# Start of a two-layer hybrid encoder: later release of the input loads, and six projections taken group by group

## What is computed

```
cond = silu(c)
mod  = cond @ w_ada[l] + b_ada[l]                    # 6 vectors of 1024 a layer: shift, scale, gate, twice
h = rms_norm(x, g_mix) * (1 + scale) + shift         # x: 2048 x 1024 a core, float32
q_a, k_a, v_a, q_b, k_b, v_b, f, q_c, k_c, v_c, gates = split(h @ w_in)
o_a = sliding-window attention with sinks and ALiBi (8 query heads, 2 key/value heads)
o_b = forgetting attention;  o_c = chunked attention with relative bias
x += gate * ((sigmoid(gates) * branch projections).sum() @ w_out)
h = rms_norm(x, g_ffn) * (1 + scale) + shift
x += gate * (silu(h @ w1) * (h @ w2)) @ w_ffn_out
```

## Time and profile before

| | |
|---|---|
| median of 3 runs (lowest to highest) | 2981.44 us (2753.49 to 3167.28) |
| the profiled execution, its own time | 2753.0 us |
| its span, slowest core (7) | 2751.4 us |
| spans of the eight cores | 2743.5 to 2751.4 us |
| TensorE, matmul busy | 2623.9 us (95%) |
| VectorE, ScalarE, POOL busy | 958.1, 984.3, 276.2 us |
| mean granted TensorE clock, core 7 | 0.982 |

### The profile page before, as it was taken

The page is one execution under the profiler, slowest core; times in us unless marked ns, Lnnn a source line. Parts: engine busy times, 40 slices in busy tenths (PEclk is TensorE's granted clock), DMA queues, the critical chain, the costliest instruction groups (busy, mean ns, idle before and its releaser), DMA issues.

```text
span 2751.4 us, 43022 instructions; the slowest of 8 cores (2743.5 to 2751.4 us)
## 1 busy us (share of the span) xinstructions
PE 2623.9 (95%) x16192; PEld 1197.6 (44%) x16192; DVE 958.1 (35%) x1423; ACT 984.3 (36%) x1326; POOL 276.2 (10%) x338
## 2 busy tenths in 40 slices
PE   1799999999999999999989999999999999999998
PEld 0234444454444444444434344454544444444443
DVE  1453221223444623223254422222244453232326
ACT  1356666554222520110143665654522243101012
POOL 1401000000000210000030100000000021000002
PEclk7799999999999999999999999999999999999999
DMA  9022222221233453343441100112032243222213
GB/s 214 16 35 48 44 48 38 54 30 18 35 45 65 111 88 64 51 76 59 70 140 25 20 13 17 18 41 41 15 50 35 41 115 62 39 39 39 39 31 123
DMA packets 66520, 148.11 MB, mean 54 GB/s; under 512 B 6592, under 2 KB 19456, under 8 KB 64272
## 3 DMA queue, kind: packets, MB, share of 16 engines
q0 software_dynamic: 55712, 99.76, 23.1%
q1 hardware_dynamic: 10608, 45.61, 4.7%
HBM read 228.12 MB, written 16.97 MB: 89 GB/s over the span
## 4 chain that ended last, share of the span: by engine, by line
PE 91%; DMA 3%; ACT 2%; DVE 2%; issue 2%; DVEq 0%; POOL 0%; POOLq 0%; ACTq 0%
PE ps L378 71%; PE ps L376 20%; DMA sb_WS<-wada 2%; ACT sb_PT L388 1%; DVE sb_TMPF L397 1%; ACT sb_HT L388 1%; DVE sb_XT L397 0%; DMA sb_WS<-win 0%; DMA sb_WS<-wfi 0%; DVE sb_RD L392 0%; ACT sb_TMPF L388 0%; ACT sb_RS L388 0%; DVE sb_W L401 0%; DVE sb_W L407 0%; ACT L388 0%
## 5 line engine op out<-in xcount | busy, mean ns | idle before, releaser
L378 PE MATMUL ps<-sb_HT,sb_WS 128*128 128x512 bf16 (+1 forms) x5760 | 1318.5, 383 | 43.0 <-ACT sb_HT L388 24.8
L378 PEld LDWEIGHTS ps<-sb_HT,sb_WS 128*128 128x128 bf16 (+1 forms) x5760 | 551.0, 98 | 725.0 <-issue 94.0
L388 ACT ACTIVATE sb_TMPF<-ps 128x512 f32<-128x512 f32 x388 | 231.6, 598 | 1140.8 <-PE ps L378 1137.4
L388 ACT ACTIVATE sb_PT<-ps 128x1024 bf16<-128x1024 f32 (+1 forms) x494 | 489.0, 990 | 404.3 <-PE ps L376 400.7
L378 PE MATMUL ps<-sb_W,sb_WS 128*128 128x512 bf16 x1920 | 418.0, 379 | 0.8 <-DVE sb_W L392 0.7
L392 DVE TENSOR_TENSOR sb_W<-ps,sb_TMPF 128x512 bf16<-128x512 f32 x176 | 121.4, 691 | 484.7 <-PE ps L378 472.7
L378 PEld LDWEIGHTS ps<-sb_W,sb_WS 128*128 128x128 bf16 x1920 | 187.5, 98 | 226.8 <-issue 1.8
L376 PE MATMUL ps<-sb_W 128*128 128x512 bf16 (+7 forms) x1212 | 256.1, 337 | 0.0
L407 DVE CAST sb_W<-ps 128x512 bf16<-128x512 f32 (+1 forms) x176 | 121.5, 690 | 386.0 <-PE ps L378 385.5
L397 DVE SCALAR_TENSOR_TENSOR sb_XT<-ps,sb_modT,sb_XT 128x512 f32<-128x512 f32 x256 | 186.5, 749 | 153.9 <-PE ps L378 153.7
L376 PE MATMUL ps<-sb_PT,sb_W 128*64 128x512 bf16 (+3 forms) x1212 | 197.0, 351 | 8.9 <-ACT sb_PT L388 7.6
(11 more groups left out here) (55 smaller groups left out, 1176.8 us busy)
## 6 DMA issues: line engine op xcount, KB each, us to landing
sb_WS<-wada POOLq DMA_DIRECT2D x48, 512.0 KB, 7.9
sb_WS<-wfi POOLq DMA_DIRECT2D x44, 512.0 KB, 5.3
sb_WS<-wmg POOLq DMA_DIRECT2D x48, 384.0 KB, 4.9
sb_XT<-x SPq DMA_DIRECT2D x8, 2048.0 KB, 18.2
sb_WS<-win POOLq DMA_DIRECT2D x60, 256.0 KB, 4.3
sb_WS<-wfo POOLq DMA_DIRECT2D x24, 512.0 KB, 5.3
xs<-sb_XT SPq DMA_DIRECT2D x4, 2048.0 KB, 6.6
sb_XT<-xs SPq DMA_DIRECT2D x4, 2048.0 KB, 17.1
```

Of the source, the lines that this page charges most:

```text
L378: r = e.matmul(o, lhsT=l, rhs=rr, start=st, stop=sp)
L388: return P.op("act", lambda e, o=out, i=in_, f=func, kw=kw: e.activation(out=o, in_=i, func=f, **kw), reads=reads, writes=writes)
```

## The change

Two things in one. First, the loads of x1, x2 and x3 no longer wait for the weights of blocks 4, 5 and 6 but all three for those of block 7, the eighth; SP issues them one behind the other. Second, `a_begin` takes all six units and `a_group` runs all six on a group, so K and V of a group come right after its Q and `a_rest` is gone. In layer 0 the norm of the next group is emitted inside the group: after the fourth projection in group 0, after the second in groups 1 and 2. In layer 1 no norm is emitted inside; group 3's norm still follows the first `a_group`, which is now six projections long. The six weights keep their order in the ring.

```diff
     def a_begin(l):
...
-        pro = [(c,) + w3(l * 30 + c, c > 0) for c in range(4)]
+        pro = [(c,) + w3(l * 30 + c, c > 0) for c in range(6)]
         return pro
...
-    def a_group(pro, g):
+    def a_group(pro, g, at=None, then=None):
         for (c, wv3, wb) in pro:
             bi = dbank()
-            drain(proj_fm(wv3, wb, g, bi))
-            ts(QA[:, c, sl(g)], PS[bi][:, :], 0.125, ALU.mult, [psb[bi]], [qab[c][g]])
-
-    def a_rest(l):
-        wv3, wb = w3(l * 30 + 4)
-        for g in range(NG):
-            bi = dbank()
-            drain(proj_fm(wv3, wb, g, bi))
-            copy("dve", KA[:, sl(g)], PS[bi][:, :], [psb[bi]], [kab[g]])
-        wv3, wb = w3(l * 30 + 5)
-        for t4 in range(4):
-            drain(proj_v(wv3, wb, t4, VA, vab, dbank()))
+            if c < 5:
+                drain(proj_fm(wv3, wb, g, bi))
+                if c < 4:
+                    ts(QA[:, c, sl(g)], PS[bi][:, :], 0.125, ALU.mult, [psb[bi]], [qab[c][g]])
+                else:
+                    copy("dve", KA[:, sl(g)], PS[bi][:, :], [psb[bi]], [kab[g]])
+            else:
+                drain(proj_v(wv3, wb, g, VA, vab, bi))
+            if c == at:
+                then()
...
     for jb in range(8):
         ada_block(0, jb)
-        if jb in (4, 5, 6):
+        if jb == 2:
+            norm_rs(0, sq)
+        if jb == 7:
             after = Buf()
             after.last_write = wsb[jb % NS].last_write
-            xload(jb - 3, x_d, [after])
-        if jb == 2:
-            norm_rs(0, sq)
+            for g in range(1, NG):
+                xload(g, x_d, [after])
...
-        a_group(pro, g)
-        if g + 1 < NG:
-            norm_fin(g + 1, sq, *mixv(0), pool=True)
+        a_group(pro, g, 3 if g == 0 else 1 if g + 1 < NG else None,
+                lambda g=g, sq=sq: norm_fin(g + 1, sq, *mixv(0), pool=True))
...
     for l in range(nl):
-        a_rest(l)
         run_steps(a_steps(l), a_filler(l), 104)
```

## The result

The changed kernel took 2721.22 us (median of 4 runs, 2720.34 to 2721.65). Of the runs of the kernel before, some were slowed by a lower clock on one die and are left out of every comparison; the undisturbed ones lie at 2751 to 2755. The ratio of after to before is 0.988, 95% interval 0.9856 to 0.9904: about 32 us faster, inside 2% and clear of no change. The profiled execution took 2720.9 us, its slowest core (2) 2719.3.

A forecast was written before the change was run, and what follows sets the result against it. Waits for conditioning weights, then idle or half-clock gaps at A's norms, were taken to bound the start. Block 7's 17.7 us and 14.8 from projections in the gaps gave -32.5: 2753.0 to 2720.5, say 2721 us, range 2709 to 2743.

The forecast's parts named there:

- Step 1, block 7: Before A: without x beside the conditioning weights, block 7 moves from 60.74 to 43 us, -17.7 (bounds -14.7 and -18.9).
- Step 1, x1's flight: Load of x1, issued at block 7's start: lands 16.5 us later, with 12 us as the other bound.
- Step 2, group 0: A's first group, us after block 7: first sum as if at +20.0, K and V hidden, second sum at +34.6.
- (b): A's own weights starve while x flows: fourth weight at +30, first sum 11.7 us later, time 2733 us; chance 0.09.
- the best case of 109: Whole phase: block 7 at 41.8, x1 after 12 us, no clock loss; phase ends at 109, time 2715 us.
- Step 2, the period: Groups 1 and 2: sums of squares 14.8 us apart instead of 19.7, TensorE idling 2.5 behind VectorE's scalings.
- The clock's term: Groups 1 and 2: 0.8 us of clock loss for two gaps of 2.5 us, bounds 0 and 5.2.
- Step 3: End of the A phase, a_rest gone: lost cover for memsets and loads costs nothing, 2 us if it fails.
- Step 4: Layer 1, six projections per group: the 8.22 us wait for a weight stays; effect 0, bounds -1 and +3 us.
- (a): x1 lands with x2 and x3, at +28 instead of +16.5; first sum onward 11.7 us later, 2733 us; chance 0.16.
- (c): Gain given back: x and weights still end at about 71, new gaps at half clock; 2744 to about 2753; chance 0.09.
- (d): Slower: x1 lands later as eight cores ask for 6 MB each at once; 2764 us if it takes 60; chance 0.04.

The follow-up runs named there:

- e3_stagger: The kernel after, but only x1 released by block 7; x2 held until K's weights have landed, x3 until V's; 2717.4 us (ratio 0.9874).
- e1_release_only: The kernel before with x1 to x3 all released by block 7, A's projections in the old order; 2735.8 us (ratio 0.9941).

## Why the prediction held, and where it did not

The forecast was 2721 us from the profiled execution's 2753.0; measured were 2721.2, and -32.5 us for the phase stands against -31.6 in the mean of the cores. Sign and place were right, and the period of groups 1 and 2 was right in its mechanism. The close size is in part luck: two terms were off and did not show.

The step that failed is the last of the sum: "A measurement of this kernel can tell about 2% (55 us) from no change, so the whole gain lies inside it." It took the 32 us that the steps before it had added up for no measurable change, and no row was given for the 2%. The runs showed that those of one kernel agree to 0.15% (2750.8 to 2754.7 for the kernel before, 2720.3 to 2721.7 for the kernel after), that the interval of the ratio is 0.5% wide (0.9856 to 0.9904), and that 1.2% is far outside it. The chance for "within 2%" held only because the gain is under that bound. Step by step:

- **Step 1, block 7.** Forecast at 43 from bounds of 41.8 to 46; measured 42.5 in the mean. The step was -17.7 on paper and is -16.1, since the core that was read had block 7 2.2 us later than the mean of the eight in the kernel before. That 43 was met is partly luck. The forecast gave three blocks 9 us from block 4's run at 33.94. They took 11.7 in the mean, 3.9 a block, which is the upper bound's 4.0 a landing and not the rate of q0 alone (7.9 for the three); but block 4 ran at 30.8 in the mean instead of 33.94. Block 5 came 5.4 us behind block 4, blocks 6 and 7 each 3.2 behind the one before.
- **Step 1, x1's flight.** I took the measured 16.5 us; it was 12.8 (12.6 to 13.2 over the cores), near the other bound. Term mis-sized by 3.7 us. Before, the shortest x load took 15.5 to 16.5 on every core, so it was not the core. A full weight queue and another x load close behind were there in both kernels and do not explain it. What differs is what the x queue had moved when x1 landed: 3.15 MB from 38 on before, 2.38 from 46 on after. Why more of x2 went ahead of x1's last piece before stays open.
- **Step 2, group 0.** With x1 early, the first sum ran at +15.5, not +20.0, and so K and V did meet their weights: V started at +27.9, where the sixth weight was forecast at +28, K at +20.3, where the fifth was forecast at +21. The second sum was forecast at +34.6 and came at +34.7, but for another reason: on paper the last HT tiles of group 1 (+31.4) set it, in the run the sixth weight did, HT being ready at +26.9. The missed 4.5 us were hidden behind a term that was right; that too is luck. "Both are hidden" was wrong of the weights: e3_stagger shows the 3.5 us that lay there, and that I had put under rival (b) without pricing it. For the same reason the best case of 109 was not consistent with the rest: with the sixth weight at +28 and no loss of clock the phase ends at +69.8, 111.6 with block 7 at 41.8.
- **Step 2, the period.** 14.8 us forecast between second and third sum, 14.7 measured on core 2, with the gap of 2.4 ended by VectorE as described. The clock's term of 0.8 for two gaps was too small on four of eight cores, where one gap cost about 1.6; it lay within the bounds of 0 and 5.2.
- **Step 2, a missed wait.** Group 2's third projection waits 0.90 us for the bank that Ln still reads, a wait that I left out.
- **Step 3.** The memsets ended at 107.3 and wf's load was issued at once, 5.4 us before the phase's end; after it TensorE went on as before. Nothing was to pay.
- **Step 4.** Forecast 0, bounds -1 and 3. The wait for win is 7.9 to 9.9 us over the cores after, 7.5 to 9.0 before; the wait stayed, as forecast. That it could be removed for 13 us I did not ask.

Of the rivals, (a) fell: three loads issued together landed at 12.8, 20.1 and 27.0 us, in their order. (b) was there in a mild form, 7.5 us of waits for win, of which only 3.5 to 4 counted. Its fuller form, a Q weight that is late, shows on single cores only: 0.94 us on core 7 of the kernel after, 0.74 on core 3 of e1_release_only. (c) fell: the phase ended at 114.0, and the stretch behind it kept its length in the mean of the cores (2601.8 and 2602.8; on the slowest cores, by which the forecast had put it at 2604, it is 2603.9 and 2606.6). (d) fell with x1's flight.

## What to carry to other kernels

In a start that is bound by transfers the total of bytes is fixed, and what can be won is their order: price each early release by what it delays, with the rate of the delayed queue alone and beside the other. Work that has its operands (here K and V) belongs in the gap between a norm's sum and its tiles, and then ask which instruction on the evacuating engine stands in front of the bank that is wanted next. A load issued on a queue that also computes waits for that computation: the largest saving found on top of the change, 13 us, was the order of four loads and four squares on POOL.

## What the runs showed of the hardware that was not expected

- A gap of 2.38 us on TensorE cost clock on some cores and not on others in the same execution: 16 matmuls took 3.61 us on core 2 and 5.29 on core 1 after the same gap. Of the six cores with a gap of 2.38 or 2.39 two lost clock (1 and 4), and so did the two with 2.68 and 2.76 (0 and 6); but in e3_stagger core 0 did not after 2.59. Gaps of 0.9 us cost nothing on any of the eight cores, and one of 9.86 lowered the granted clock to 0.71 of full speed in the 7.2 us behind it.
- Three 2 MB loads issued within 1.6 us on one queue landed one after the other, 7 to 8 us apart. Whether the two others stood behind it or not, x1 took about as long beside a full weight queue: 12.8 us in the kernel after, 12.9 in e3_stagger. A later load of e3_stagger took 8.1 on the core where x1 took 12.9, when the weight queue moved 0.02 MB from 57 to 59 and nothing after.
- With x in 2 KB rows instead of 16 KB, issued in 24 pieces, the x queue moved 5.30 MB from 46 to 68 against 6.19. From 50 to 54 the weight queue moved 0.27 MB against 0.12, and the turns were not one to one.
